# Expert products with stationary operands of 128 columns, 128 words apart, and bias rows packed for them

## The reference, cut to what matters

```python
def moe_ffn(h, router_w, router_b, w1, b1, w2, b2):
    ...
    logits = (xt @ router_w + router_b).astype(jnp.float32)
    top_val, top_idx = lax.top_k(logits, TOP_K)      # 4 of 32
    gates = jax.nn.softmax(top_val, axis=-1)
    ...
    def expert_block(args):
        tok, gate, e = args
        hid = xt[tok] @ w1[e] + b1[e]                # 1024 -> 2048
        out = clamped_swiglu(hid) @ w2[e] + b2[e]    # 1024 -> 1024
        return out * gate[:, None].astype(out.dtype)
```

## Time and profile before

| | |
|---|---|
| median of 3 runs (lowest, highest) | 1637.74 us (1637.68, 1638.72) |
| the profiled execution: its time, its span | 1644.19 us, 1642.4 us |
| PE busy, PEld busy | 1575.4 us (96%), 1155.0 us (70%) |
| DVE, ACT, POOL busy | 1332.3 us (81%), 1019.0 us (62%), 601.7 us (37%) |
| first and last matmul of the expert blocks | from 469 us to 1620 us |
| read from DRAM | 443.67 MB, of which 384 loads of 1 MiB are expert weights |

### The profile page before, as it was taken

The page is one execution under the profiler, slowest core; times in us unless marked ns, Lnnn a source line. Parts: engine busy times, 40 slices in busy tenths (PEclk is TensorE's granted clock), DMA queues, the critical chain, the costliest instruction groups (busy, mean ns, idle before and its releaser), DMA issues.

```text
span 1642.4 us, 23296 instructions
## 1 busy us (share of the span) xinstructions
PE 1575.4 (96%) x7924; PEld 1155.0 (70%) x7924; DVE 1332.3 (81%) x1169; ACT 1019.0 (62%) x881; POOL 601.7 (37%) x398
## 2 busy tenths in 40 slices
PE   6999989999989999999999999999999999999994
PEld 5777788886566677777777777777777777777773
DVE  4499766443578889999899899899989999989994
ACT  4534333320366677777777777777777777776774
POOL 5643512322331214444333434433433433333431
PEclk9999989999989999999999999999999999999997
DMA  5322101111469999999999999999999999999994
GB/s 175 129 77 78 15 13 52 53 52 36 180 244 316 384 376 374 374 376 381 376 376 377 372 374 379 381 371 379 379 365 379 380 379 377 379 371 372 390 388 150
DMA packets 146547, 467.15 MB, mean 284 GB/s; under 512 B 21014, under 2 KB 35004, under 8 KB 146428
## 3 DMA queue, kind: packets, MB, share of 16 engines
q1 hardware_dynamic: 136684, 437.36, 70.8%
q0 software_dynamic: 9664, 28.53, 7.4%
q10 hardware_dynamic: 144, 0.52, 0.1%
HBM read 443.67 MB, written 22.71 MB: 284 GB/s over the span
## 4 chain that ended last, share of the span: by engine, by line
PE 82%; DVE 10%; DMA 3%; issue 2%; ACT 2%; SPq 0%; DVEq 0%; POOLq 0%; ACTq 0%
PE banks L1702 21%; PE banks L1704 21%; PE banks L1703 21%; PE banks L1647 3%; DMA slots<-in_expert_w_dram 2%; PE banks L1711 2%; PE banks L1731 1%; PE banks L1534 1%; PE banks L1697 1%; PE banks L1544 1%; DVE lo L2057 1%; PE banks L1350 1%; PE banks L1351 1%; PE banks L1352 1%; PE banks L1446 1%
## 5 line engine op out<-in xcount | busy, mean ns | idle before, releaser
L2057 DVE TENSOR_TENSOR lo<-slots,hi 128x2048 fp32r<-128x2048 f32 x384 | 863.0, 2286 | 52.4 <-PE banks L1704 43.9
L1133 ACT CAST hi<-slots 128x2048 fp32r<-128x2048 f32 x384 | 734.0, 1912 | 249.2 <-PE banks L1704 132.5
L1702 PE MATMUL banks<-lo,x_hi 128*96 128x512 f32 x1040 | 414.6, 399 | 0.0
L1704 PE MATMUL banks<-hi,x_lo 128*96 128x512 f32 x1040 | 409.9, 394 | 0.0
L1703 PE MATMUL banks<-hi,x_hi 128*96 128x512 f32 x1040 | 409.0, 393 | 0.0
L915 POOL DMA_INDIRECT x_sum<-hT,idy x32 | 89.6, 2801 | 461.3 <-ACT hT L1222 446.8
L1704 PEld LDWEIGHTS banks<-hi,x_lo 128*96 128x96 f32 x1040 | 168.5, 162 | 73.7
L940 POOL COPY idx_all<-ovf_pair 96x2 int32 x28 | 164.1, 5860 | 153.3 <-DMA ovf_pair<-slot_tokens,ovf_col 153.3
L1703 PEld LDWEIGHTS banks<-hi,x_hi 128*96 128x96 f32 x1040 | 169.0, 162 | 68.7
L1702 PEld LDWEIGHTS banks<-lo,x_hi 128*96 128x96 f32 x1040 | 168.5, 162 | 68.0
L1702 PE MATMUL banks<-lo,a_hi 128*96 128x512 f32 x496 | 196.1, 395 | 2.1 <-DVE lo L2057 2.1
(11 more groups left out here) (372 smaller groups left out, 1906.4 us busy)
## 6 DMA issues: line engine op xcount, KB each, us to landing
slots<-in_expert_w_dram SPq DMA_DIRECT2D x384, 1024.0 KB, 10.7
slots<-in_w_in_dram SPq DMA_DIRECT2D x13, 1024.0 KB, 5.2
xs<-in_x_dram SPq DMA_DIRECT2D x8, 512.0 KB, 5.8
slots<-in_w_out_dram SPq DMA_DIRECT2D x2, 2048.0 KB, 7.8
x_sum<-xs SPq DMA_DIRECT2D x4, 512.0 KB, 13.9
h_rows<-slots SPq DMA_DIRECT2D x4, 512.0 KB, 2.6
xs<-x_sum SPq DMA_DIRECT2D x4, 512.0 KB, 5.0
x_sum<-xs POOLq DMA_DIRECT2D x3, 512.0 KB, 10.1
```

The costliest lines, as they stand in the source:

```text
L1133: nc.scalar.copy(w_hi[n % HI][:, :, :], raw[r]).then_inc(hi_ready, 1)
L1702: nc.tensor.matmul(out, x_h, w_l, start=first, stop=False)
L1704: return nc.tensor.matmul(out, x_l, w_h, start=False, stop=last)
L2057: tensor_tensor(w_lo[n % LO][:, :, :], raw[n % RAW], w_hi[n % HI][:, :, :], ALU.subtract).then_inc(lo_ready, 1)
```

## The change

The stationary buffers `x_hi`, `x_lo`, `a_hi` and `a_lo` get 128 columns for each slice instead of 96, so that slice k begins 128·k words into its buffer. The data still fill the first 96 columns; columns 96 to 127 are zeroed once. The matmuls load all 128 columns and write all 128 rows of the PSUM bank. `sel` becomes 128 columns wide too, in two forms for each block. The bias table is packed: 1024 columns instead of 2048, with the rows of the second 512-column piece of each half lying below those of the first (rows 64 to 127), so that bank c of a half takes the same 512 columns of `b1r` with its own form of `sel`. To make room, `a_hi`, `squares` and `fox_rms_of` move to other buffers.

```diff
-        squares = region(BKf, 2 * D, D)
+        squares = region(ARf, D, D)
...
-        x_hi, x_lo = (rounded(f"x_{nm}", "BK", BW, o, [P, KT, NS]) for nm, o in (("hi", 3 * CW), ("lo", 3 * CW + KT * NS)))
-        a_hi = rounded("a_hi", "BK", BW, 3072, [P, FT, NS])
-        sel = rounded("sel", "BK", BW, 3072 + FT * NS, [P, 2, NS])
-        a_lo = rounded("a_lo", "hT", BW, 3 * D, [P, FT, NS])
-        b1r = rounded("b1r", "qk", BW, 2 * D, [P, F2])
+        x_hi, x_lo = (rounded(f"x_{nm}", "BK", BW, o, [P, KT, P]) for nm, o in (("hi", 3 * CW), ("lo", 3 * CW + KT * P)))
+        sel = rounded("sel", "BK", BW, 3 * CW + 2 * KT * P, [P, 2, 2, P])
+        a_hi = rounded("a_hi", "qk", BW, 3 * D, [P, FT, P])
+        a_lo = rounded("a_lo", "hT", BW, 3 * D, [P, FT, P])
+        b1r = rounded("b1r", "qk", BW, 2 * D, [P, 2, CW])
+
+        def slots_of(t):
+            return t[:, :, 0:NS].rearrange("p (b k) s -> p b k s", b=2)
...
             for g in range(2):
-                sp.dma_start(biasrows[g * E:(g + 1) * E, :], b1[0]).then_inc(bias_in, 16)
+                for c in range(2):
+                    sp.dma_start(biasrows[(2 * c + g) * E:(2 * c + g + 1) * E, :].rearrange("e (h w) -> e h w", h=2),
+                                 b1[0].rearrange("e (h c w) -> e h c w", h=2, c=2)[:, :, c]).then_inc(bias_in, 16)
...
-            nc.gpsimd.memset(biasrows[2 * E:P, :], 0.0).then_inc(bias_zeroed, 1)
...
-                        nc.scalar.copy(b1r[:, :], biasrows).then_inc(bias_split, 1)
+                        nc.scalar.copy(b1r[:, :, :], biasrows.rearrange("p (h w) -> p h w", h=2)).then_inc(bias_split, 1)
...
-                nc.scalar.copy(x_hi[:, :, :].rearrange("p (b k) s -> p b k s", b=2), first_turned if first else turned)\
+                nc.scalar.copy(slots_of(x_hi), first_turned if first else turned)\
...
                 if u % 4 == 0:
-                    for c in range(2 * half, 2 * half + 2):
-                        nc.tensor.matmul(bank[2 + c][0:NS, :], sel[:, q, :], b1r[:, c * CW:(c + 1) * CW], start=True, stop=False)
+                    for c in range(2):
+                        nc.tensor.matmul(bank[2 + 2 * half + c], sel[:, q, c, :], b1r[:, half, :], start=True, stop=False)
                 for k2 in range(2):
                     k = u % 4 * 2 + k2
                     for c in range(2):
-                        ins = three_products(bank[2 + 2 * half + c][0:NS, :], x_hi[:, k, :], x_lo[:, k, :],
+                        ins = three_products(bank[2 + 2 * half + c], x_hi[:, k, :], x_lo[:, k, :],
                                              w_hi[n % HI][:, 2 * k2 + c, :], w_lo[n % LO][:, 2 * k2 + c, :], k == KT - 1)
...
-                        ins = three_products(bank[first_bank + h][0:NS, :], hi[:, f, :], lo[:, f, :],
+                        ins = three_products(bank[first_bank + h], hi[:, f, :], lo[:, f, :],
...
-                nc.vector.tensor_copy(sel[:, q, :].unsqueeze(2), expert_row[:, bass.ds(e, 1)].unsqueeze(1).to_broadcast([P, NS, 1]))\
+                nc.vector.tensor_copy(sel[:, q], expert_row[:, :, bass.ds(e, 1)].to_broadcast([P, 2, P]))\
...
-                        tensor_tensor(b1r[E:2 * E, :], biasrows[E:2 * E, :], b1r[E:2 * E, :], ALU.subtract).then_inc(bias_split, 1)
+                        for r in (slice(E, 2 * E), slice(3 * E, 4 * E)):
+                            tensor_tensor(b1r[r], biasrows[r].rearrange("p (h w) -> p h w", h=2), b1r[r], ALU.subtract)\
+                                .then_inc(bias_split, 1)
...
                     if st == ("o", 1, 1):
                         dve.wait_ge(g2_in, 16)
+                        for t in (x_hi, x_lo, a_hi):
+                            step(nc.vector.memset(t[:, :, NS:].bitcast(f32), 0.0))
                         set_expert(0, 0)
                         set_expert(1, 1)
...
             x_low(0, True)
+            step(nc.vector.memset(a_lo[:, :, NS:].bitcast(f32), 0.0))
```

More of the change, by code:

```diff
@@ L193, in hymba_layer @@
         outb = [region(hTf, 3072, D), region(hTf, 0, D), region(hTf, D, D), region(ARf, 2 * D, D)]
-        biasrows = region(ARf, 0, F2)
+        biasrows = region(ARf, 0, 2 * CW)
         VR = {}
@@ L216, in hymba_layer @@
         rb = sb("rb", [P, E])
-        expert_row = sb("expert_row", [P, E])
+        expert_row = sb("expert_row", [P, 2, E])
         fb = sb("fb", [H, 1])
@@ L244, in hymba_layer @@
         fst = sb("fst", [P, H])
-        fox_rms_of = sb("fox_rms_of", [P, TT, H])
         dend = sb("dend", [P, JT, NC])
@@ L270, in hymba_layer @@
         pos = sb("pos", [P, TT, E])
+        fox_rms_of = pos[:, 0, :].rearrange("p (t h) -> p t h", t=TT)
         slotm = sb("slotm", [P, TT, E])
@@ L394, in hymba_layer @@
         g2_in = sem("g2_in")
-        bias_zeroed = sem("bias_zeroed")
         bias_raised = sem("bias_raised")
@@ L887, in _ @@
             pool.dma_start(idx_all[:, 0:E, :], slot_tokens[0:NS * E, :].rearrange("(s e) a -> s e a", e=E)).then_inc(idx_in, 16)
-            pool.wait_ge(bias_split, 2)
+            pool.wait_ge(bias_split, 3)
             pool.wait_ge(idx_in, 16)
@@ L1174, in _ @@
                         act.wait_ge(bias_raised, 1)
-                        act.wait_ge(bias_zeroed, 1)
-                        nc.scalar.copy(b1r[:, :], biasrows).then_inc(bias_split, 1)
+                        nc.scalar.copy(b1r[:, :, :], biasrows.rearrange("p (h w) -> p h w", h=2)).then_inc(bias_split, 1)
                     if st[2] == 1:
@@ L1215, in act_high @@
                 act.wait_ge(at_full, b + 1)
-                nc.scalar.copy(dst[:, :, :].rearrange("p (b k) s -> p b k s", b=2), turned).then_inc(a_hi_ready, 1)
+                nc.scalar.copy(slots_of(dst), turned).then_inc(a_hi_ready, 1)
             def scale_rows(q, b, stores, i, n_after, src=y_banks):
@@ L2095, in _ @@
             dve.wait_ge(consts_ready, 4)
-            step(tensor_tensor(expert_row[:, :], ident[:, 0:E], ident[:, E:2 * E], ALU.add))
+            for c in range(2):
+                step(tensor_tensor(expert_row[:, c, :], ident[:, 2 * c * E:(2 * c + 1) * E],
+                                   ident[:, (2 * c + 1) * E:(2 * c + 2) * E], ALU.add))
             tensor_tensor(rw[:, :, :], rw[:, :, :], vec("g2").unsqueeze(2).to_broadcast([P, KT, E]), ALU.mult).then_inc(rw_ready, 1)
@@ L2194, in _ @@
                     if st == ("o", 2, 0):
-                        dve.wait_ge(bias_in, 16 * 8)
-                        tensor_scalar(biasrows[0:2 * E, 1:F2:2], biasrows[0:2 * E, 1:F2:2], 1.0, None, ALU.add)\
+                        dve.wait_ge(bias_in, 16 * 10)
+                        tensor_scalar(biasrows[:, 1:2 * CW:2], biasrows[:, 1:2 * CW:2], 1.0, None, ALU.add)\
                             .then_inc(bias_raised, 1)
@@ L2239, in x_low @@
                 dve.wait_ge(x_hi_ready, b + 1)
-                tensor_tensor(x_lo[:, :, :].rearrange("p (b k) s -> p b k s", b=2), first_turned if first else turned,
-                              x_hi[:, :, :].rearrange("p (b k) s -> p b k s", b=2), ALU.subtract).then_inc(x_lo_ready, 1)
+                tensor_tensor(slots_of(x_lo), first_turned if first else turned, slots_of(x_hi), ALU.subtract).then_inc(x_lo_ready, 1)
             def act_low(b, lo=a_lo, hi=a_hi):
                 dve.wait_ge(a_hi_ready, b + 1)
-                tensor_tensor(lo[:, :, :].rearrange("p (b k) s -> p b k s", b=2), turned,
-                              hi[:, :, :].rearrange("p (b k) s -> p b k s", b=2), ALU.subtract).then_inc(a_lo_ready, 1)
+                tensor_tensor(slots_of(lo), turned, slots_of(hi), ALU.subtract).then_inc(a_lo_ready, 1)
             def swiglu(b, p, first=False):
```

## The result

The changed kernel took 1626.28 us, the median of 4 runs (1624.80 to 1627.85), beside 1637.87 us for the kernel before on the same chip (1637.68 to 1638.72, 4 runs). The ratio is 0.9933, with a 95% interval of 0.9918 to 0.9948: faster by 11.6 us (0.7%) between the medians, by 8.5 to 13.4 us over the interval. The forecast was 17.8 us less. Its direction holds, and the time lies within the outer bounds of 1616 to 1638.5, but 2 us outside the forecast's own range of 1616 to 1624 and close to the 1628 that the transfers' rival gave for half the rise in rate. In a later group of runs the same changed kernel came to 0.9909 (0.9894 to 0.9924), 1623.87 us against 1639.19, and beside a further group to 0.9924 (0.9910 to 0.9937), 1630.38 us against 1641.62.

A forecast was written before the change was run, and what follows sets the result against it. PE was taken as the bound, with DMA engines nearly full too. 19.4 us from intervals, less 0.6 for early blocks, set-up 0, less 1 for waits: 17.8 us, so 1620 us; own range 1616 to 1624, outer 1616 to 1638.5.

The forecast's parts named there:

- the transfers' rival: Weight blocks: full DMA engines hold the block at 35.5 us; 1636 us, or 1628 if the rate rises halfway; 27 in 100.
- The product's interval: Expert products on PE: start-to-start time falls from 0.2308 to 0.2267 us, as in the input projection.
- The formula weighed there: PE matmuls: gap N / 2.4 + 2.5, 215.7 ns for 512, whatever the stationary operand; the change would be worth nothing.
- an interval that doesn't move: Expert products: interval stays 0.2308 us, time 1637.7 plus or minus 1.5 for the set-up; 15 in 100.
- one that grows: Expert products: interval rises towards the b2 product's 0.235 us, time up to 1657.6 us; 8 in 100.
- The sum of the intervals: All PE products: 4736 intervals x 4.1 ns = 19.4 us; per block 148, 0.61 us, so 34.89 for 35.50.
- The early blocks: First 2 blocks, where PE waits for others: a faster PE may gain nothing, 0.6 us counted as lost.
- Late waits reaching PE: Blocks: weight loads landing late make ACT wait, and some waits now reach PE; 1 us taken off.
- The transfers as the bound: Blocks: DMA engines at full share cannot exceed 377 GB/s where 384 is needed; some 2 us gained, 1636; 27 in 100.
- DVE and the set-up: DVE in a block: `sel` at most 0.33 us more, free; set-up memsets and bias between -1.3 and +1.5 us, taken as 0.

The follow-up runs named there:

- wide96: Changed kernel with 128 columns loaded but slices still 96 words apart: 1638.70 us against 1638.64 for the kernel before, ratio 1.0000.
- half loads: Half of each weight load left out: changed kernel 1618.34 us, kernel before 1631.76, both against 1638.64 for the unaltered kernel before.
- the repeat: The changed kernel unaltered, run once more in a later group: 1623.87 us against 1639.19 for the kernel before, ratio 0.9909.
- after_beside: The changed kernel unaltered, run and profiled again in a further group: 1630.38 us against 1641.62 for the kernel before, ratio 0.9924.

## Why the prediction was right in direction and too large

**The product's interval: right.** The new operands start 0.227 us apart and load in 189 ns. Of the three rows between which I chose, the input projection's was the right one. The reason I gave for it, rows, columns and spacing together, has been taken apart since: width and a start on a multiple of 64 words (as against 32 words past one) are both needed. The spacing of 128 words matters only as it gives every slice such a start, which is what wide96's own slices 0, 2, 4 and 6 show. The formula weighed there (Trainium skill, TensorE: Matmul & The Clock Gate, Back-to-back issue gap) lets the interval depend on the moving size alone; that section gives it for an isolated matmul and says that in a stream of weight loads and matmuls both set the spacing, without a term for width or start. As a price for this stream the trace disagrees with the formula: 226.7, 230 and 233 ns for the same 512 moving columns. The rivals of an interval that doesn't move and of one that grows are out, though the latter was real in a place: operands that start 32 words off take 233.

**The sum of the intervals: the step that failed.** I multiplied 4.1 ns by all 148 intervals of a block, which is 0.61 us; it is 0.48 (35.50 to 35.02). The missing 0.13 us lie behind the transposes. Twice in a block eight of them run, and the first interval after them was 291 ns and is 314, by about as much as the load got longer (27 ns, 189 for 162); that the load is no longer hidden there is my reading, not shown. It follows the width, not the spacing: 292 with 96 columns 128 words apart, 315 with 128 columns 96 words apart. The next five intervals were 229 to 233 and are still 228 to 236, so they don't take part in the gain. The mean of the six went from 241.0 to 245.5 ns where I had counted on 236.9: 8.6 ns x 12 = 0.10 us, and the three after them, still at 228 to 231, add a few hundredths. Over the 29 steady blocks of the profile the gain is 13.9 us where the same step made it 17.7. That the earlier trace rows showed only undisturbed intervals, while a block has 16 transposes in it, stood in the prediction (1.3 us "with their transitions"), and I took those as fixed.

**The early blocks: mis-sized.** I had taken off 0.6 us and so assumed that they merely wouldn't gain; they took 0.4 more in the profile (80.28 for 79.88). The direction of the reasoning, PE waits for others there, is shown by the half loads (74.5 us, with no wait of PE for `lo`). But I read only the waits in the earlier trace rows and not the granted clock in the same row, 0.96: of the two blocks' 80 us some 4 are the clock at half, a term that the prediction doesn't have.

**Late waits reaching PE: mis-sized.** I took off 1 us. In the profile the 27 blocks from 572.76 to 1520.92 us took 948.16 us, 27 x 35.02 is 945.5: 2.6 us; the block at 1520.92 lost another 1.8. That is 4.4 us by the way foretold (a load lands late, ACT, then DVE, then PE), but it was 0.9 us in the repeat, 3.8 in `after_beside`, and 0.2 with an eighth of the bytes left out. The sum of the profile's stretches that can be the change's: -13.9 + 4.4 + 0.4 = -9.1 us, to which the set-up adds between 0 and -0.9, so about -10; the measured -11.6 (8.5 to 13.4) agrees. For the repeat, -13.9 and some 1 us of waits, and early blocks at 76.7 for 79.9: -16, beside a ratio that says -15. These 3.2 us of the early blocks are the clock's, which never fell there in that execution: luck of the execution, not the change.

**The transfers as the bound: partly right.** The blocks at 35.02 need 383 GB/s, and the engines carried it. The full share did not mean what it says. But the waits of ACT nearly doubled, from 101 to 194 us, and in some executions part of them reaches PE, in others hardly any.

**DVE and the set-up: right.** `sel` takes 279 ns for 196 (I had allowed up to 0.52), DVE is busy 32.57 us in a block for 32.52. The memsets took 0.27 us each, and between the two kernels with half loads the start of the two early blocks differs by less than 1 us.

## What to carry to other kernels

Give a stationary operand all 128 columns and start every slice of it on a multiple of 64 words, with zeroed columns as filling if there are too few; either alone moved the interval by a fifth of it or by nothing. Only starts on a multiple of 64 words and 32 words past one were measured. When you price a faster instruction, count only the instances that follow their own kind: those behind a switch (here the transposes) may get slower, as here, where the load had become longer. And look at a nearly full resource in the stretch where it already makes others wait, and there at the granted clock too: a wait of PE can be followed by a slower stretch that costs nearly as much again.

## What the runs showed of the hardware that I had not expected

A matmul of 512 moving columns in this format, each with a new stationary operand, takes 226.7 ns with 128 columns and a start on a multiple of 64 words, 230.1 ns with 96 columns and a start on a multiple of 128, 230.9 with 96 columns 96 words apart, and with 128 columns that start 32 words off 232.5 to 232.8 on the mean, up to 241 for the first of a slice. Why the start counts is not shown; no run here looks inside.

With a share of 1.02 to 1.03 the DMA engines moved anything from 353 (the first two blocks) to 382 GB/s over whole blocks, and 390 and 392 in the earlier trace rows. The Trainium skill (DMA: Bandwidth & Descriptors, Where 436 GB/s comes from) names about 358 GB/s as the limit of the DRAM side for a core, worked out as half of what two cores share. Only the first two blocks of two profiles lie near it with 353 and 354 (371 in the repeat); the steady ones are above, and so contradict it as a limit for a single core that runs alone. What makes one execution carry 383 GB/s without a gap in PE, and another 380 with gaps, stays open.
